# Last attention pass: score groups of 512, 1024 and 768 keys, a second bank for the first group, one bank for turned mixes, weighted products spread over the step, attention output on ScalarE

## The reference, cut to what matters

```
def diff_attn_block(q, k, v, lam):
    s = jnp.einsum('bqhnd,bkhnd->bnhqk', q, k).astype(jnp.float32) * (1.0 / math.sqrt(HEAD_DIM))
    a = jax.nn.softmax(s, axis=-1)
    a = a[:, 0] - lam * a[:, 1]
    return jnp.einsum('bhqk,bkhv->bqhv', a.astype(v.dtype), v)
...
attn = (rms_norm(attn, subln_g) * (1.0 - lam_i)).reshape(B, T, ATTN_WIDTH)
```

## Time and profile before

| | us |
|---|---|
| median of 3 runs | 3195.71 (3194.67 to 3197.0) |
| the profiled execution | 3194.44 |
| its span | 3192.6 |
| PE busy | 3088.7 (97%) |
| DVE busy | 2240.2 (70%) |
| ACT busy | 1609.1 (50%) |

### The profile page before, as it was taken

One profiled execution on the slowest core, in us unless ns is written; L12 is line 12 of the kernel. 1 busy time (PEld: TensorE's weight loads), 2 busy tenths in 40 slices (PEclk: granted clock), 3 DMA queues, 4 the chain that ended last, 5 costly groups with the idle time before them and its releaser, 6 DMA issues. The chain is left out here.

```text
span 3192.6 us, 67289 instructions
## 1 busy us (share of the span) xinstructions
PE 3088.7 (97%) x22490; PEld 2804.0 (88%) x22490; DVE 2240.2 (70%) x3960; ACT 1609.1 (50%) x3558; POOL 698.0 (22%) x902
## 2 busy tenths in 40 slices
PE   7989999999999999998999997999999999999999
PEld 5989989998998998997887776999999999989998
DVE  5888878888887887887994557555555555555554
ACT  4656666666666665665771225333434333333332
POOL 2532233333333333232210002111111111111111
PEclk9999999999999999999999997999999999999999
DMA  8754344335335435344335556566555555555664
GB/s 292 260 198 123 126 132 143 116 120 156 120 116 156 121 123 158 120 128 137 120 121 191 197 184 204 193 198 198 185 185 185 185 185 185 185 185 185 198 200 132
DMA packets 341255, 530.37 MB, mean 166 GB/s; under 512 B 29690, under 2 KB 256250, under 8 KB 325882
## 3 DMA queue, kind: packets, MB, share of 16 engines
q1 hardware_dynamic: 330956, 493.47, 47.0%
q0 software_dynamic: 10160, 35.13, 4.4%
HBM read 439.10 MB, written 88.64 MB: 165 GB/s over the span
## 5 line engine op out<-in xcount | busy, mean ns | idle before, releaser
L3173 PE MATMUL ps_gu<-xT,e_w 128*128 128x272 f32 x6144 | 775.9, 288 | 0.2 <-DVE xT L3371 0.2
L3173 PEld LDWEIGHTS ps_gu<-xT,e_w 128*128 128x128 f32 x6144 | 772.2, 188 | 1.6 <-issue 0.3
L1228 ACT ACTIVATE e<-ps_s,negm 128x1024 f32<-128x1024 f32 (+2 forms) x416 | 474.2, 1145 | 241.1 <-DVE negm L1631 200.5
L1616 DVE TENSOR_REDUCE mx<-ps_s 128x1 f32<-128x1024 f32 (+3 forms) x428 | 526.0, 1232 | 66.4 <-PE ps_s L849 62.4
L849 PE MATMUL ps_s<-kT,qT 128*128 128x512 f32 (+1 forms) x1920 | 478.0, 386 | 14.4 <-ACT e L1228 13.3
L3360 DVE TENSOR_TENSOR e_w<-e_raw,e_w 128x2048 fp32r<-128x2048 f32 x126 | 288.5, 2289 | 207.6 <-ACT e_w L3231 207.6
L849 PEld LDWEIGHTS ps_s<-kT,qT 128*128 128x128 f32 x1920 | 341.6, 190 | 86.8 <-ACT e L1228 29.3
L926 PE MATMUL ps_m<-w,hT 128*128 128x384 f32 x2040 | 391.6, 340 | 3.9 <-DVE o L1683 3.9
L891 PE MATMUL ps_m<-v,aT 128*128 128x128 f32 x2816 | 370.0, 278 | 1.2 <-ACT aT L1212 1.2
L926 PEld LDWEIGHTS ps_m<-w,hT 128*128 128x128 f32 x2040 | 348.9, 189 | 5.4 <-issue 5.4
L891 PEld LDWEIGHTS ps_m<-v,aT 128*128 128x128 f32 x2816 | 340.2, 193 | 5.2 <-ACT aT L1212 2.9
(11 more groups left out here) (439 smaller groups left out, 4188.6 us busy)
## 6 DMA issues: line engine op xcount, KB each, us to landing
hT<-hT_d SPq DMA_DIRECT2D x85, 1024.0 KB, 5.3
e_raw<-w_gate SPq DMA_DIRECT2D x48, 1024.0 KB, 5.2
e_raw<-w_up SPq DMA_DIRECT2D x48, 1024.0 KB, 7.5
e_raw<-w_down SPq DMA_DIRECT2D x32, 1024.0 KB, 14.6
e_raw_more<-w_down SPq DMA_DIRECT2D x32, 1024.0 KB, 7.5
tab<-tabs_d SPq DMA_DIRECT2D x85, 256.0 KB, 2.7
hT_d<-hT SPq DMA_DIRECT2D x17, 1024.0 KB, 3.9
w_lent<-w_ada SPq DMA_DIRECT2D x16, 1024.0 KB, 5.5
```

Source lines behind the costliest of these rows:

```text
L1228: nc.scalar.activation(out, src, ACT.Exp, bias=negm[:, s.par, c:c + 1], scale=HD ** -0.5, accum_out=acc).then_inc(exp_done.sem, 1)
L1616: nc.vector.tensor_reduce(mx[:, c, n:n + 1], ps_s[:, at:at + hi - lo], AX, ALU.max).then_inc(mx_part.sem, 1)
L3173: mm = nc.tensor.matmul(ps_gu[:, 2 * (s % 2) + f, 0:SLOTS], w_view(s, a)[:, k, f * P:f * P + P], xT[:, b, k, :], start=(k == 0 and a + b = ...
```

## The change

In the last pass the three key groups are 512, 1024 and 768 wide. The first group of map c = 1 goes to the second bank of `ps_t` (`score_at`), and in exchange all turned chunks share the first bank (`turn_bank`), so that each `turn` waits for the copy of the chunk before. ACT takes the exponentials in the order group 1, 0, 2. The scores of group 0, map 0 of the next tile are computed in the step before. `weighted(p, 2)` and `turn(p, 3)` move into the next step, and the weighted products stand apart. `evacuate`, `normal_out` and the high part of `split_out` move from DVE to ACT.

```diff
-    LAST_GROUPS = ((0, 1024), (1024, 2048), (2048, KEYS))
+    LAST_GROUPS = ((0, 512), (512, 1536), (1536, KEYS))
+        def exp_order(s):
+            return (1, 0, 2) if s.front == "sample" and s.h == H else range(len(groups_of(s)))
+        def score_at(s, c, n):
+            if s.front != "sample":
+                return ps_s[:, 1024 * c:1024 * c + P]
+            if late(s) and c == 1 and n == 0:
+                return ps_t[:, 1, :]
+            lo, hi = groups_of(s)[n]
+            return ps_s[:, lo:hi]
+        def turn_bank(s, n):
+            return 0 if late(s) else n % 2
...
@@ PE: scores, the wait ahead of a group
+                    last_pass = s.h == H and s.front == "sample"
+                    if late(s) and last_pass and n == 0:
+                        if c == 1:
+                            exp_done.wait(pe, s, -1)
+                        else:
+                            exp_done.wait(pe, s, -4 if late(previous(s)) else -1)
...
+                    elif last_pass and c == 1:
+                        exp_done.wait(pe, s, (2, 1, 3)[n])
+                    elif late(s) and last_pass:
+                        exp_done.wait(pe, s, (0, -2, 0)[n])
@@ PE: turn
+                elif late(s):
+                    aT_act.wait(pe, s, n)
                 elif n >= 2:
                     aT_act.wait(pe, s, n - 1)
...
-                    mm = nc.tensor.transpose(ps_t[:, n % 2, m * P:m * P + P], src[:, b * P:b * P + P], g.ident[:])
+                    mm = nc.tensor.transpose(ps_t[:, turn_bank(s, n), m * P:m * P + P], src[:, b * P:b * P + P], g.ident[:])
@@ PE: late_body (the order itself stands in the rows below)
@@ ACT: new functions
+            def evacuate(s):
+                pv_part.wait(act, s, 5)
...
+                nc.scalar.activation(o[:], ps_m[:, 0:P], ACT.Copy, scale=rl[:, s.prev_par, 0:1]).then_inc(o_done.sem, 1)
+            def normal_out(s):
+                orr_done.wait(act, s, 1)
...
+                nc.scalar.activation(on[:], o[:], ACT.Copy, scale=orr[:]).then_inc(on_done.sem, 1)
+            def high_out(s):
...
+                nc.scalar.activation(cat[:, s.par, 0, :], out_at(s), ACT.Copy, scale=sg[:]).then_inc(o_hi.sem, 1)
@@ ACT: late_body
-                exps(s, 0, slice(0, 1))
-                if late(previous(s)):
-                    square_out(previous(s))
-                exps(s, 0, slice(1, None))
-                if s.j is not None or s.i < NS:
+                p = previous(s)
+                exps(s, 0, slice(0, 2))
+                if late(p):
+                    evacuate(p)
+                exps(s, 0, slice(2, None))
+                if s.i < NS:
                     keep_half(s)
-                for n in range(3):
-                    copy_turned(s, n)
-                exps(s, 1, slice(0, 2))
+                copy_turned(s, 0)
+                if late(p):
+                    square_out(p)
+                copy_turned(s, 1)
+                if late(p):
+                    normal_out(p)
+                exps(s, 1, slice(0, 1))
+                copy_turned(s, 2)
+                exps(s, 1, slice(1, 2))
+                if late(p):
+                    high_out(p)
                 copy_turned(s, 3)
                 exps(s, 1, slice(2, None))
                 copy_turned(s, 4)
@@ DVE: late_body
                 negate(s, 0)
+                maximum(s, 1, 0)
                 if late(p):
-                    evacuate(p)
                     coefficient(s)
                     mix(s, 0)
                     mix(s, 1)
-                    mean_square(p)
                 mix(s, 2)
-                for n in range(len(groups_of(s))):
+                for n in range(1, len(groups_of(s))):
                     maximum(s, 1, n)
                     if n == 1:
                         fold(s, 1)
+                        if late(p):
+                            mean_square(p)
...
                 negate(s, 1)
-                if late(p):
-                    normal_out(p)
                 mix(s, 3)
                 mix(s, 4)
                 first_sums(s)
                 if late(p):
-                    split_out(p)
+                    low_out(p)
```

More of the change, by code:

```diff
@@ L818, in scores @@
                         mod2_done.wait(pe, s, 1)
-                    if c == 1 and s.front == "sample":
+                    last_pass = s.h == H and s.front == "sample"
[4 more added lines that the diff above has]
+                            exp_done.wait(pe, s, -4 if late(previous(s)) else -1)
+                        if s.i == 1 and c == 1:
+                            kq_copied.wait(pe, s)
+                            aT_act.wait(pe, s)
+                    elif last_pass and c == 1:
+                        exp_done.wait(pe, s, (2, 1, 3)[n])
+                    elif late(s) and last_pass:
+                        exp_done.wait(pe, s, (0, -2, 0)[n])
+                    elif c == 1 and s.front == "sample":
                         exp_done.wait(pe, s, n + 1)
@@ L834, in scores @@
                     stationary = qT[:, s.par] if s.front == "sample" else qTp[:, head % 2]
-                    at = lo if s.front == "sample" else 1024 * c
+                    out = score_at(s, c, n)
                     parts_of = [(lo, min(lo + 1024, hi)), (min(lo + 1024, hi), hi)]
@@ L848, in scores @@
                                 keys = kT[:, head % 2, c, x:y] if s.front == "sample" else kTp[:, head % 2, c, :]
-                                mm = nc.tensor.matmul(ps_s[:, at + x - lo:at + y - lo], lhs, keys, start=(half == 0),
+                                mm = nc.tensor.matmul(out[:, x - lo:y - lo], lhs, keys, start=(half == 0),
                                                       stop=(half == 1))
@@ L1094, in late_body @@
                 p = previous(s)
-                scores(s, 0, slice(0, 1))
+                ahead = s.front == "sample" and s.i + 1 < NS
+                if s.front == "sample":
+                    if not late(p):
+                        scores(s, 0, slice(0, 1))
+                    scores(s, 0, slice(1, 2))
+                if late(p):
+                    weighted(p, 2)
+                    turn(p, 3)
+                if s.front == "sample":
+                    scores(s, 0, slice(2, None))
                 if late(p):
                     turn(p, 4)
-                scores(s, 0, slice(1, None))
+                if s.front != "sample":
+                    scores(s, 0)
+                scores(s, 1, slice(0, 1))
                 if late(p):
                     weighted(p, 3)
+                if s.i < NS:
+                    modulation_half(s)
+                if late(p):
                     weighted(p, 4)
-                if s.j is not None or s.i < NS:
-                    modulation_half(s)
-                scores(s, 1, slice(0, 1))
+                scores(s, 1, slice(1, 2))
                 turn(s, 0)
+                scores(s, 1, slice(2, None))
+                weighted(s, 0)
                 turn(s, 1)
-                scores(s, 1, slice(1, None))
-                weighted(s, 0)
+                if ahead:
+                    scores(Slot(H, s.i + 1), 0, slice(0, 1))
                 turn(s, 2)
                 weighted(s, 1)
-                weighted(s, 2)
                 if late(p):
@@ L1218, in exps @@
                 coef_done.wait(act, s, 0)
-                for n, (lo, hi) in list(enumerate(groups_of(s)))[some]:
+                for n in exp_order(s)[some]:
+                    lo, hi = groups_of(s)[n]
                     if n == 2 and c == 0:
@@ L1224, in exps @@
                     if s.front == "sample":
-                        out, src, acc = e[:, s.par, c, lo:hi], ps_s[:, lo:hi], l3[:, s.par, c, n:n + 1]
+                        out, acc = e[:, s.par, c, lo:hi], l3[:, s.par, c, n:n + 1]
                     else:
-                        out, src, acc = ep[:, c, :], ps_s[:, 1024 * c:1024 * c + P], l3p[:, c, 0:1]
-                    nc.scalar.activation(out, src, ACT.Exp, bias=negm[:, s.par, c:c + 1], scale=HD ** -0.5,
+                        out, acc = ep[:, c, :], l3p[:, c, 0:1]
+                    nc.scalar.activation(out, score_at(s, c, n), ACT.Exp, bias=negm[:, s.par, c:c + 1], scale=HD ** -0.5,
                                          accum_out=acc).then_inc(exp_done.sem, 1)
@@ L1611, in maximum @@
             def maximum(s, c, n):
-                lo, hi = groups_of(s)[n]
-                at = lo if s.front == "sample" else 1024 * c
                 per = len(groups_of(s))
                 s_ready.wait(dve, s, per * c + n + 1)
-                nc.vector.tensor_reduce(mx[:, c, n:n + 1], ps_s[:, at:at + hi - lo], AX, ALU.max).then_inc(mx_part.sem, 1)
+                nc.vector.tensor_reduce(mx[:, c, n:n + 1], score_at(s, c, n), AX, ALU.max).then_inc(mx_part.sem, 1)
             def fold(s, c):
@@ L1697, in split_out, with low_out @@
                 cat_saved[s.par].wait(dve, s, 0)
```

(12 more changed lines are left out.)

12 lines of the change are left out of this document (9 added, 3 removed).

## The result

The changed kernel takes 3226.22 us (median of 4, 3223.94 to 3227.4), the kernel before 3196.36 in the same rounds: a ratio of 1.0092, interval 1.008 to 1.0104. It is slower by 30 us. The forecast was 3234, the range 3208 to 3254. The profiled execution has a span of 3225.0 us.

The account below looks back on a forecast made before the run. Steady steps were taken as about 11.7 us of PE work and 0.5 of waiting. Step ring 25.3, casts 1.6 and edges 1 gave 28 us; with 11 for the clock, 39: forecast 3234 us, range 3208 to 3254.

Parts of the forecast that it names:

- The deciding wait: PE's 768-wide scores behind turned chunk 3 wait for a copy and an exponential: 1.8 us, 1.65 without tail.
- The ring round the step: Chain through PE, ACT and DVE from one step's 768-wide scores to the next's: 14.1 us instead of 12.16, +25.3 us.
- PE's own stretch from the 768-wide scores to the evacuation: First part of the step's ring: PE's scores, turn 4, products and modulation without a wait, 4.55 us.
- The other two waits: PE waits 0.4 to 0.5 us each at the second 768-wide scores and at turn 2.
- The clock: PE falls to 1.2 GHz behind about every second new wait in the steady steps: +11 us, bounds 0 and 21.
- The rival of a full clock: PE's clock stays at 1.00 despite the new waits: 3222 us, 3223 by the median; chance 0.25.
- The casts on ACT: Eight weight-rounding casts now between the copy of chunk 4 and the next exponential: 1.6 us, bounds 0 and 8.
- The edges: First and last steps of the pass, with changed exponential order and shared turned bank: together +1 us.
- Faster by relief of DVE: Rival: the 0.5 us wait behind the modulation slice goes, ring stays under PE's work: 3188 us; chance 0.06.
- No change by give and take: Rival: the wait comes, PE's small losses between groups go in exchange: 3191 to 3201 us; chance 0.05.

Follow-up runs that it names:

- e1: The changed kernel with turned chunk 3 ahead of weighted product 2 on PE: 3212.9 us, step 13.53 us.
- e2: The changed kernel with the last exponential of a step ahead of the copy of chunk 3 on ACT: 3207.9 us, step 13.16 us.
- b4: The kernel before with the normalisation of the output alone moved to ACT: 3195.5 us, step 12.16 us.
- e8: The kernel before with only the new groups of 512, 1024 and 768 keys: 3206.8 us, step 13.06 us.
- e5: The changed kernel with output on DVE, turn 3 ahead of product 2, last exponential ahead of copy 3, turn 1 ahead of product 0: 3205.1 us.

## Why the prediction was right, and where it was off

**The deciding wait: right, in size too.** The prediction put 1.65 us ahead of the 768-wide scores, in every step from i = 2, from a copy and an exponential in series. Measured: 1.57, 13 times in 13 intervals. From start to start it is 1.73 (1561.94 to 1564.11, less 0.44 for the turning), against 1.79. e1 and e2 cut this ring at two places and each took back about what was expected of it.

**The ring round the step: right in kind, a little short.** Forecast 14.14, measured 14.40; over 13 intervals 25.3 became 29. The mis-sized term is PE's own stretch from the 768-wide scores to the evacuation. I had 4.55 us; in the rows above it is 1564.11 to 1569.02, 4.91. Of the 0.36 too little, 0.15 are PE's own rows up to the scores at 1568.74 (4.63 for 4.48; the single products take 0.98 and 0.92 instead of 0.94, the modulation slice 1.03 instead of 0.95). The other 0.21 are the end of the last product: ACT starts 0.28 behind 1568.74, when the product's row has ended (1568.98), and I had 0.07. The rest of the ring came out 0.1 shorter than its terms. The other two waits were forecast as 0.4 to 0.5 each; the profile gives 0.3, without the tail of the row before, and from start to start they are about 0.46. By the same measure PE's own work is 11.7 to 11.8 us a step, before and after, so the split groups cost PE next to nothing; they didn't in the forecast either.

**The clock: wrong.** Of the 39 us, 11 were for TensorE at 1.2 GHz behind every second wait. The steady steps ran at a granted clock of 1.00 throughout. These windows of the changed kernel hold one of the waits and what follows it:

```profile
1519.30:1522.60 3.30, 1.73 (x11) 1.54 (x11) 1.81 (x3) 1.73 (x4) 0.00 (x0) 1.00 0.38 127
1522.70:1526.00 3.30, 3.30 (x83) 3.04 (x82) 3.16 (x9) 2.28 (x6) 0.00 (x0) 1.00 0.02 5
```

PE was busy 1.73 of 3.30 us, and the clock stayed. From the two of the earlier trace rows behind which it was lost and the one behind which it was kept I took every second wait; it was none of 13. The rival of a full clock, 3222 and 3223 by the median, was the nearer one, and its chance of 0.25 was too low. By the rule of the Trainium skill (TensorE: Matmul & The Clock Gate, "Why this matters for your kernels"), that only long gaps lose the clock, the forecast would have been 3223, and on these waits the trace agrees; on the waits of 1.94 and 1.95 us in the kernel before it doesn't. Why those lost it and waits of 1.57 don't is not settled here; no run varied it.

The prediction had no term for the clock at the edges of the pass, and there it did change. The first wait grew from 1.94 us to 3.12, and the changed kernel ran 13.6 us in one piece at a granted clock of 0.50; the kernel before had three stretches of 3.4 us there. At the end the kernel before had two more, one in the earlier trace rows and one here first; the changed kernel had none:

```profile
1680.70:1684.10 3.40, 3.40 (x19) 3.40 (x18) 2.33 (x8) 1.48 (x4) 0.33 (x1) 0.50 0.02 5
```

```profile
1482.38 4.21 PE L879 MATMUL ps_s<-kT,qT 128*128 128x512 f32 x10 [3.12 <-ACT e L1275]
```

```profile
1481.80:1495.40 13.60, 10.57 (x27) 7.63 (x27) 9.81 (x24) 4.87 (x14) 2.56 (x5) 0.50 0.40 125
1700.00:1744.50 44.50, 36.98 (x211) 30.20 (x211) 21.18 (x57) 13.03 (x36) 6.15 (x17) 1.00 0.46 166
```

This goes with the 1.6 us lost up to step 2 and the 2 us given back at the end; no run parts the clock from the other changes there.

**Small terms.** The casts on ACT, put at 1.6 us, left no mark: steps with and without them are 14.38 to 14.42. The edges were put at +1; they sum to about -0.4. The first copy of the modulation slice was 2.9 us later than before, of which 2.4 had come about ahead of the pass.

**Luck.** The forecast of +39 was 9 us too high because errors of opposite sign met: 11 too much for the clock and 3 too much for the small terms, against 4 too little for the ring; the last microsecond is within what the timing can tell.

**The other rivals.** Faster by relief of DVE: excluded. b4 shows that even before, the work of DVE ahead of its maxima was not what held the step; the maxima and the bias behind them are in the chain, as the earlier trace rows and e8 show. No change by give and take: excluded, the step grew by 2.24 us.

## What to carry to other kernels

Before two instructions are put next to each other on one engine, follow what the second waits for back to its source: if the source is the first, through other engines, the whole way is idle time, and one piece of independent work between them pays it. Waits in one ring add up; taking load off an engine that is 95% busy gains nothing if the ring doesn't run through the work that is taken off. Price a new split of the work by its last group, whose exponential, scores and maximum follow each other, and not by sums. Compare PE's work from start to start: a row ahead of a wait counts its tail as busy.

## What the runs showed of the hardware

GpSimd's subtractions and VectorE's mixes, which read two operands from SBUF, slow each other: two 512-wide mixes took 1.93 to 2.38 us beside the subtractions and 1.41 alone, four subtractions 3.69 to 3.90 against 2.80; beside maxima out of PSUM neither was slowed. The Trainium skill (SBUF — State Buffer, "Who interferes with whom") has a pair of ports that the two engines hold in turn, for VectorE operations with two SBUF inputs too; that there is such a conflict, and that maxima out of PSUM are free of it, agrees with the trace. That one of the two holds them alone does not: the mixes of e5 ran from 1563.85 to 1566.23 within the subtractions' 1563.12 to 1566.81, and both went on, slower.

The evacuation of 128 columns took 0.37 us on ACT (0.27 from its start to the next operation's) and 0.35 on DVE.
